# Experts in nine weight slots, and one body for all rounds of an expert in nested fixed loops

## The reference

```python
g_star = argmax(xf @ wg + bg)                   # one of 4 groups
e_logits = (xf @ we + be)[group g_star]         # its 8 experts
top_val, top_idx = lax.top_k(e_logits, 2)       # two experts a token
gate = p_group * softmax(top_val)
y_e = (silu(x_e @ w1[e]) * (x_e @ w3[e])) @ w2[e]   # for the tokens of expert e
out = sum over the token's two experts of gate * y_e
x = layer_norm(alpha * x + out)
```

## Time and profile before

| what | value |
|---|---|
| median of 3 runs | 1573.17 us (1564.77 to 1573.19) |
| the profiled execution | 1563.52 us, its span 1561.5 us |
| granted TensorE clock over the span | 0.929 |
| TensorE matmul busy | 1202.1 us (77%) |
| weight loads of the MoE | 192 of 2 MB |
| mean DMA rate over the span | 303 GB/s |

### The profile page before, as it was taken

How to read it: one execution, slowest core, us unless ns; L and a number is a source line. 1 busy time by engine, 2 the same in 40 slices (tenths; PEclk the granted TensorE clock), 3 DMA queues, 4 the chain that set the end, 5 groups by cost and what they waited for, 6 DMA issues and landing times.

```text
span 1561.5 us, 39311 instructions
## 1 busy us (share of the span) xinstructions
PE 1202.1 (77%) x16430; PEld 843.9 (54%) x16431; DVE 385.5 (25%) x1017; ACT 155.0 (10%) x455; POOL 62.1 (4%) x88
## 2 busy tenths in 40 slices
PE   7999999966767767667669999997778666666652
PEld 6884547544545545445547866655555444444431
DVE  1863622251111111112114222252111111111113
ACT  0211401110000000000001001100000000000000
POOL 3000010010000000000001001020000000000001
PEclk9999999988999999989979999989999899998996
DMA  9655113168998999999992445134799999999992
GB/s 322 235 185 193 55 54 135 55 269 363 429 429 357 428 428 429 428 429 429 428 396 84 162 162 188 55 135 163 327 429 428 430 428 429 428 428 430 428 428 92
DMA packets 63203, 473.39 MB, mean 303 GB/s; under 512 B 4092, under 2 KB 9532, under 8 KB 38572
## 3 DMA queue, kind: packets, MB, share of 16 engines
q1 hardware_dynamic: 60940, 465.78, 72.8%
q0 software_dynamic: 2208, 6.81, 1.4%
HBM read 471.52 MB, written 1.05 MB: 303 GB/s over the span
## 4 chain that ended last, share of the span: by engine, by line
PE 51%; DMA 35%; issue 7%; DVE 5%; ACT 1%; POOL 0%; DVEq 0%; SPq 0%; POOLq 0%
DMA ring<-in_moe_w_dram 34%; PE bank L462 13%; PE bank L825 12%; PE bank L475 7%; PE bank L841 4%; PE bank L849 2%; PE bank L817 2%; PE bank L638 2%; DVE x L960 1%; DMA ring<-in_ev_w_in_dram 1%; PE bank L593 1%; PE bank L764 1%; PE bank L437 1%; PE bank L626 1%; ACT prob L1527 1%
## 5 line engine op out<-in xcount | busy, mean ns | idle before, releaser
L825 PE MATMUL bank<-ring,kT 128*32 128x128 f32 x8192 | 307.2, 316 | 217.8 <-DMA ring<-in_moe_w_dram 135.8
L825 PEld LDWEIGHTS bank<-ring,kT 128*32 128x32 f32 x8192 | 272.5, 128 | 258.4 <-DMA ring<-in_moe_w_dram 130.1
L462 PE MATMUL bank<-xT,ring 128*128 128x256 f32 x832 | 181.9, 380 | 4.2 <-DMA ring<-in_ev_w_in_dram 1.6
L462 PEld LDWEIGHTS bank<-xT,ring 128*128 128x128 f32 x832 | 158.0, 191 | 28.4 <-issue 4.7
L841 PE MATMUL bank<-ring,probT 128*32 128x256 f32 x2336 | 140.6, 381 | 32.7 <-DMA ring<-in_moe_w_dram 25.3
L1272 DVE SCALAR_TENSOR_TENSOR probT<-probT,bank 128x128 f32<-128x128 f32 x73 | 21.0, 288 | 493.9 <-ACT probT L1521 493.5
L841 PEld LDWEIGHTS bank<-ring,probT 128*32 128x32 f32 x2336 | 73.5, 109 | 93.2 <-DMA ring<-in_moe_w_dram 44.7
L475 PE MATMUL bank<-ring,oT 128*128 128x512 f32 x256 | 110.8, 593 | 3.8 <-issue 1.9
L849 PE MATMUL bank<-prob 32*128 32x256 f32 x1024 | 74.0, 400 | 32.0 <-ACT prob L1527 31.5
L475 PEld LDWEIGHTS bank<-ring,oT 128*128 128x128 f32 x256 | 48.3, 190 | 64.7 <-issue 64.7
L849 PEld LDWEIGHTS bank<-prob 32*128 32x128 f32 x1024 | 46.5, 184 | 64.6 <-ACT prob L1527 62.3
(11 more groups left out here) (268 smaller groups left out, 935.4 us busy)
## 6 DMA issues: line engine op xcount, KB each, us to landing
ring<-in_moe_w_dram SPq DMA_DIRECT2D x192, 2048.0 KB, 25.4
ring<-in_od_w_in_dram SPq DMA_DIRECT2D x6, 2048.0 KB, 16.2
ring<-in_ev_w_in_dram SPq DMA_DIRECT2D x4, 2048.0 KB, 16.4
ring<-in_xa_wq_dram SPq DMA_DIRECT2D x4, 2048.0 KB, 12.0
ring<-in_xa_wo_dram SPq DMA_DIRECT2D x4, 2048.0 KB, 11.3
ring<-in_mem_wk_dram SPq DMA_DIRECT2D x2, 2048.0 KB, 14.1
ring<-in_mem_wv_dram SPq DMA_DIRECT2D x2, 2048.0 KB, 11.2
ring<-in_ev_w_out_dram SPq DMA_DIRECT2D x2, 2048.0 KB, 7.8
```

The source lines that it names most:

```text
L462: ins = mm(ps, w[:, k, c0:c0 + P], rhs[:, k, :], start=(k == 0), stop=(k == KC - 1))
L825: ins = mm((b1, b3)[m][qs[q], 0:P], xg[:, k, :], w[:, k, q * P:(q + 1) * P], start=(k == 0), stop=(k == KC - 1))
```

## The change

- The six slots of `ring` are joined by three more, laid over buffers that are dead in the MoE: `slot6` over `qT, aT, kT, blocks`, `slot7` over `prob, probT`, `slot8` over `memT, oT`. Three sets of three slots hold three experts. Nine loads are issued ahead of the MoE loop, as each slot comes free (`xa_done` is new for `slot7`).
- The small MoE buffers (`xgT`, `hid`, `disp`, ...) move into `xT`, which is dead in the MoE.
- There is one body for all rounds of an expert, and one family of semaphores a layer. Each engine goes through two nested fixed loops (4 x 2 passes), with a test in each, in place of the first round's code and the loop of 7 passes. The next round, of whatever expert, is always gathered in the middle of the present one.
- An expert's registers `m` (its rounds) and `first` (the rounds ahead of it) are loaded before its rounds. They come from `units`, which is made by a comparison, a reduction and two small matmuls instead of the prefix sum.
- The tail behind TensorE's loop is gone: the loop has 11 turns of 3 experts, with an empty 33rd expert. The loop's first instruction is put on the start of a block of instructions (`head_slot`).

```diff
-                with pe.Fori(0, TURNS - 1) as i:
-                    for j in range(SETS):
-                        expert(i, j, False)
-                for j in range(SETS):
-                    expert(TURNS - 1, j, j == SETS - 1)
+                def unit(s, ready, n):
+                    pe.wait_ge(fam.gathered, n)
+                    pe.wait_ge(loaded[s[0]], ready[0])
+                    hidden(fam, 0, s[0], xgT)
+                    pe.wait_ge(loaded[s[1]], ready[1])
+                    hidden(fam, 1, s[1], xgT)
+                    pe.wait_ge(fam.disp_gated, n)
+                    turn(fam, dispg)
+                    pe.wait_ge(fam.disp_built, n + 1)
+                    gather(fam, disp)
+                    ...
+                    results(fam, s[2])
+                    pe.wait_ge(fam.y_ready, n)
+                    scatter(fam, comb, y)
+                with nc.Fori(0, TURNS, engines=[pe.engine], head_slot={pe.engine: 0}) as i:
+                    for j in range(SETS):
+                        m, first = load_units(pe, L, i * SETS + j)
+                        ...
+                        with pe.Fori(0, ROUNDS // 2) as ra:
+                            with pe.If(m > ra * 2):
+                                with pe.Fori(0, 2) as rb:
+                                    with pe.If(m > ra * 2 + rb):
+                                        unit(s_, ready, first + ra * 2 + rb + 1)
+                                    pe.nop()
                             pe.nop()
```

The same on VectorE, and SP's loads:

```diff
+                with v.Fori(0, NE) as e:
+                    m, first = load_units(v, L, e)
+                    with v.Fori(0, ROUNDS // 2) as ra:
+                        with v.If(m > ra * 2):
+                            with v.Fori(0, 2) as rb:
+                                with v.If(m > ra * 2 + rb):
+                                    r = ra * 2 + rb
+                                    n = first + r
+                                    with v.If(n > 0):
+                                        v.wait_ge(fam.disp_gated, n)
+                                        build(e, r)
+                                        elements(n)
+                                        v.wait_ge(fam.comb_done, n)
+                                        v.wait_ge(fam.gather_done, n + 1)
+                                        take(fam, xgT)
+                                    v.nop()
+                                    v.wait_ge(fam.disp_built, n + 1)
+                                    weight(e)
+                def next_expert(e, j):
+                    m, first = load_units(sp, L, e)
+                    for m_ in range(3):
+                        s = slots[j][m_]
+                        sp.wait_ge(used_up[m_], first + m)
+                        sp.dma_start(slot_ap(s), expert_weights(PARTS[m_], L, e + SETS)).then_inc(loaded[s], 16)
```

The routing's end on VectorE and TensorE:

```diff
-                st.do(ts(counts[:, 1, :], counts[:, 0, :], float(CAP), None, ALU.is_gt))
-                ... (the prefix sum of L1312 to L1322)
+                st.do(tt(beyond[:, :], banks[7][0:NE, 0:ROUNDS], round_caps[0:NE, :], ALU.is_gt))
+                nc.vector.tensor_reduce(units_of[:, :], beyond[:, :], AX, ALU.add).then_inc(units_of_ready, 1)
+                v.wait_ge(fam.gather_done, 1)
+                take(fam, xgT)
+                v.wait_ge(first_ready, L + 1)
+                cp(units[0:1, L, :, 0:NE], ...).then_inc(units_ready, 1)
...
+                pe.wait_ge(units_of_ready, L + 1)
+                mm(bY[0:1, 64:64 + NE], units_of[:, :], ident[0:NE, 0:NE], start=True, stop=True)
+                mm(bY[0:1, 64 + NE:64 + 2 * NE], units_of[:, :], tri[0:NE, 0:NE], start=True, stop=True).then_inc(first_ready, 1)
+                pe.wait_ge(units_ready, L + 1)
```

More of the change, by code:

```diff
@@ L242, in program @@
         mask_ready = sem("mask_ready")
-        rounds_ready = sem("rounds_ready")
-        held_over = sem("held_over")
-        shift_done = [sem(f"shift_done{L}") for L in range(DEPTH)]
+        xa_done = sem("xa_done")
+        counted = sem("counted")
+        units_of_ready = sem("units_of_ready")
+        first_ready = sem("first_ready")
+        units_ready = sem("units_ready")
         class Family:
@@ L307, in wait_drained, with load_units @@
             eng.wait_ge(bank_drained[b], n)
[L309 to L314, removed]
+        def load_units(eng, L, e):
+            at_ = bass.ds(e, 1) if not isinstance(e, int) else slice(e, e + 1)
+            m = eng.value_load(units[0:1, L, 0, at_], min_val=0, max_val=ROUNDS)
+            first = eng.value_load(units[0:1, L, 1, at_], min_val=0, max_val=UNITS - 1)
+            return m, first
         block = ctx.enter_context(nc.Block())
@@ L322, in _, with wait_free @@
             at = [0]
+            def wait_free(s):
+                last = slot_last[s]
+                if last is None:
+                    return
+                if len(last) == 2:
+                    sp.wait_ge(last[0], last[1])
+                else:
+                    m, first = load_units(sp, last[1], last[2])
+                    sp.wait_ge(last[0], first + m)
             def load(key, dst_view, src):
@@ L326, in load @@
                 at[0] += 1
-                last = slot_last[s]
-                if last is not None:
-                    sp.wait_ge(last[0], last[1])
+                wait_free(s)
                 slot_uses[s] += 1
@@ L387, in _ @@
                     load_out(f"xo{L}{'ab'[h]}", T["xa_wo"][L], 512 * h)
[L389 to L392, removed]
+                free = [(at[0] + k) % RING for k in range(RING)]
+                slots = ((free[0], free[1], 6), (free[2], free[3], 7), (free[4], free[5], 8))
@@ L393, in _ @@
+                moe_slots.append(slots)
                 moe_base.append(list(slot_uses))
-                sp.wait_ge(rounds_ready, L + 1)
-                e0 = L * NE
-                with sp.Fori(1, TURNS) as i:
-                    for j in range(SETS):
[L399 to L405, removed]
@@ L406, in _ @@
-                for j in range(SETS):
[L407 to L414, removed]
+                slot_last[6] = (weights_used, order.index(f"wo_mix{L}b") + 1)
@@ new lines, in _ @@
+                sp.wait_ge(units_ready, L + 1)
+                with sp.Fori(0, TURNS - 2) as i:
+                    for j in range(SETS):
+                        next_expert(i * SETS + j, j)
+                for e in range((TURNS - 2) * SETS, NE - SETS):
+                    next_expert(e, e % SETS)
+                for e in range(NE - SETS, NE):
+                    for m_ in range(3):
+                        s = slots[e % SETS][m_]
+                        slot_uses[s] += e // SETS + 1
+                        slot_last[s] = (used_up[m_], L, e)
@@ L777, in _ @@
                     wait_drained(pe, ("xo", L, h))
+                pe.nop().then_inc(xa_done, 1)
                 out_projection(f"xo{L}", 3 * L + 1)
@@ L851, in scatter @@
                     ins.then_inc(fam.scattered, 1)
-                e0 = L * NE
+                fam = families[L]
                 for t in range(TT):
                     pe.wait_ge(x_ready[t], 3 * L + 2)
[L856 to L887, removed]
-                                    pe.wait_ge(main.gathered, n1 + 1)
-                                pe.wait_ge(fam.disp_built, k1)
-                                gather(fam, more_disp)
-                                pe.wait_ge(fam.gathered, k1)
-                                hidden(fam, 0, 3 * j, more_xgT)
-                                hidden(fam, 1, 3 * j + 1, more_xgT)
-                                pe.wait_ge(fam.disp_gated, k1)
-                                turn(fam, more_dispg)
-                                pe.wait_ge(fam.comb_ready, k1)
-                                pe.wait_ge(fam.hidT_ready, k1)
-                                results(fam, 3 * j + 2)
-                                pe.wait_ge(fam.y_ready, k1)
-                                scatter(fam, more_comb, more_y)
-                            pe.nop()
-                        pe.nop()
@@ L1303, in _ @@
                 st.wait()
-                v.wait_ge(main.disp_built, e0 + 1)
-                weight(main, disp, dispg, 0)
-                v.wait_ge(main.gather_done, e0 + 1)
-                take(main, xgT)
-                v.wait_ge(main.disp_gated, e0 + 1)
-                build(main, disp, place_of(place, 1))
-                wait_drained(v, ("pos", L))
-                st.do(ts(counts[:, 1, :], counts[:, 0, :], float(CAP), None, ALU.is_gt))
-                for r_ in range(2, ROUNDS):
-                    st.do(stt(out=counts[:, 1, :], in0=counts[:, 0, :], scalar=float(r_ * CAP), in1=counts[:, 1, :], op0=ALU.is_gt, op1=ALU.add))
@@ L1369, in _ @@
-                with v.Fori(0, TURNS - 1) as i:
-                    for j in range(SETS):
-                        expert(i, j, 2)
-                for j in range(SETS):
-                    expert(TURNS - 1, j, SETS - 1 - j)
```

(5 more changed lines are left out.)

231 lines of the change are left out of this document (108 added, 123 removed).

## The result

The changed kernel takes 1658.12 us (median of 4 runs, 1648.38 to 1661.0) against 1572.66: the ratio is 1.055 (95% interval 1.051 to 1.060), slower. Its profiled execution has a span of 1646.4 us against 1561.5, 84.9 more.

What follows compares the result with a forecast made beforehand. Weight transfers were taken to bound the MoE, TensorE being only a little faster; after the change TensorE would, at 15.7 us an expert. Layer 0 +63 and layer 1 +47 on 1563.5 gave 1673, stated as 1675 us, range 1590 to 1725.

Steps and rivals of the forecast that it cites:

- A failing pass: On TensorE's queue, one loop pass whose test fails (add, move, two taken branches) costs 0.735 us; four per one-round expert.
- From `scatter` to `hidden`: TensorE's control between experts, first `scatter` matmul to next `hidden`: 6.73 us, against 2.2 before.
- The slow round: TensorE's way from `hidden` to `scatter` takes 8.95 us instead of 7.29, its clock being lower after each longer gap.
- An expert 15.7 us: TensorE's time per one-round expert, 8.95 + 6.73 us, over the weights' 14.67; bounds 15.2 to 16.4.
- A further round: Another round of the same expert on TensorE costs 7.6 us, following at once; before, 9.85 plus failing passes of 4.4.
- Loop ends: Behind each layer's last expert: loop ends 4 us and an instruction fetch 3.3 us before the first matmul after the loop.
- The routing: Before each layer's experts, TensorE's wait for `units_ready`, loads and loop entries delay first `hidden` by 2.3 us; VectorE adds 4 in layer 0.
- The third set: Nine weight loads instead of six ready when routing ends: 43 + 22 = 65 us to be had if weights stayed the bound.
- Rival (a): TensorE's rounds keep the upper clock, 14.0 us an expert: 1568 us, no change; chance 0.12.
- Rival (b): TensorE's queue hides the control, gap under 3 us, expert under 12, weights stay the bound: 1498 us; chance 0.10.
- Rival (c): Instruction fetches in the expert loop, one miss of 3.3 us an expert, 211 us more: 1885 us; chance 0.06.
- the two rules: Skill's rules set against the trace: a taken branch costs about 108 ns (trace 0.214 us); far branches fetch (none in steady loops).

Runs made afterwards that it cites:

- e3_eight_outer: Changed kernel with TensorE's outer loop at 8 passes instead of 4, the four more always failing; 1847.37 us (one run).
- e4_fill: Changed kernel with three bf16 matmuls on zeros, results unused, at the end of every outer pass of TensorE; 1548.32 us, ratio 0.992.
- e1_loop_of_m: Changed kernel with TensorE's nested loops replaced by one loop of exactly m passes, other engines keeping theirs; 1501.97 us, ratio 0.961 to the kernel before.
- e5_two_sets: e1_loop_of_m with two sets of three slots instead of three; 1526.11 us, ratio 0.975 to the kernel before.
- e6_before_passes: Kernel before the change plus a loop of five failing passes on TensorE at the end of every expert; 1597.33 us, ratio 1.022.

## Why the prediction was right, point by point

The sign, the mechanism and the size held (1675 forecast, 1658 measured, in the range). The sum is 25 us too high: it has 110 us more than before, and the spans are 84.9 apart. Some terms missed in opposite directions.

- *A failing pass, 0.735 us*: confirmed, 0.74 to 0.75 by e3_eight_outer. The changed kernel's own records have the outer passes from 434.4 to 436.7, three periods.
- *From `scatter` to `hidden`, 6.73 us*: 5.96 and 6.00 (means of 31 in each layer). The sum took too much for arithmetic and for the entries: `ra * 2` has no instruction of its own but lies in the one fused record a pass (41 ns), which the price of a pass already holds, so the term of 0.5 comes to nearly nothing, and the entries into both loops took 0.64 (438.5 to 439.1) where the sum has 0.84. Over 62 experts the 0.75 are 46 us.
- *The slow round, 8.95 us*: too low. The first rounds of the experts take 9.32 and 9.33 (means of 32 in each layer); with the further rounds, which follow at once at 7.29, the mean is 9.05 and 9.11. They alternate between 8.6 and 9.9. Over 62 experts the 0.37 are 23 us, which offset half of the item above: that the sum came so near is in part luck. e4_fill shows that it is the clock. The trace of before had shown it only behind further rounds; that the same gap does it every time was the step that carried the sign, and it held.
- *An expert 15.7 us*: 15.4, from `hidden` to `hidden` (mean of the 54 experts that have one round and another expert behind them). The 0.3 x 62 = 19 us cover the 17 by which the two loops are shorter than the sum has them (533.2 and 526.9 against 543.4 and 533.3). The other 8 of the 25 lie outside the loops, where the sum has 4.6 more than before and the trace 3.7 less; the routing did cost about what was forecast (below), and what else moved there stays open.
- *A further round, 7.6 us*: 7.6. The five experts with two rounds in layer 0 take 23.03 us on average (22.74 for expert 8, from 455.15 to 477.89), less the 15.4 of one that has a single round.
- *Loop ends, 4 + 3.3 us*: 8.2 (856.68 to 864.91). The empty 33rd expert, whose loads and failing passes I forgot, is in it.
- *The routing, +2.3 us in each layer*: from the mask's matmul to the first `hidden` 6.88 us (324.81 to 331.69), 4.62 before (327.42 to 332.04): +2.26; in layer 1 it is +2.0. The +4 for VectorE's loops in layer 0 did not come: `gather` waits 0.75 us for `build`, no more, since `build` ran at 337.90 already. That step was wrong. So was the -1.5 and -1.3 for a warm expert 0: its first `hidden` took 5.37 us in both layers, behind 3.64 and 3.36 us of idle time.
- *The DMA share about 0.93*: 0.91 in layer 0. *Waits for weights vanish*: they did.
- *The third set, 65 us to be had*: e1_loop_of_m gave 62 against the kernel before, but e5_two_sets gives only 24 of it to the set. The prediction put the whole under the third set; most of it comes from the rest of the change.
- *Rival (a), rounds at the upper clock, 1568*: that is what e4_fill forces, 1548: lower since the gap is 6.05 us there and not 6.73. *Rival (b), 1498*: not what happens, but its arithmetic is e1_loop_of_m's 1502. *Rival (c)*, fetches in the loop: none seen. The 10 us that the range allowed for first visits did not come either: behind the first three experts the ways from `scatter` to `hidden` are 6.07, 6.09 and 6.35 us. The kernel before had 8.58 and 9.96 behind its first two, part of what the one body saves.
- On the two rules: the taken compare-and-branch is 0.214 us in the changed kernel as well, not the 108 ns of the Trainium skill (Advanced Engine Details and Errata, Control Flow Timing).

The matmuls of the routing's start, of after:

```profile
324.81 0.41 PE L827 MATMUL bank<-mask,tri 128*128 128x32 f32 x2 [0.31 <-DVE mask L1265]
...
338.18 1.07 PE L848 MATMUL bank<-x,xT 128*32 128x256 f32 x16 [0.75 <-DVE xT L1276]
```

and of before:

```profile
327.42 0.41 PE L798 MATMUL bank<-mask,tri 128*128 128x32 f32 x2 [0.31 <-DVE mask L1248]
```

## What to carry to other kernels

Count the branches on the engine that has the least room, not the instructions saved: here one taken branch on TensorE's queue is 0.27 us from its record to the next, so one an expert is worth 0.27 us x 64 = 17 us when TensorE is the bound, and none of it is in the busy times. A loop of exactly as many passes as there is work replaces tests that fail. And price the idle time that control opens by the clock it costs as well as by itself: a gap of 5 us made the next 7.3 us of work take 9.3 on average.

## What the runs showed of the hardware that was not expected

- Gap and slow rounds go together in steps. With 2.3 to 2.7 us from `scatter` to `hidden` (idle 1.1 to 1.6) rounds stay at 7.29; at 4.5 (idle 3.3) nearly all are near 8.9, a few at 9.4 to 9.6; at 6.0 (idle 4.8 to 5.2) they alternate between 8.6 and 9.9, in two kernels of quite different code. With 8.9 (e3_eight_outer) it is no worse: first rounds of 9.3 and 9.2 us on average. e6_before_passes lies in between: its gaps alternate between 3.8 and 4.3 us (idle 2.6 and 3.1), and in the middle of layer 0 the rounds behind the shorter ones mostly take 7.29 us, those behind the longer ones 8.95 and more:

```profile
535.18 3.70 PE L825 MATMUL bank<-ring,kT 128*32 128x128 f32 x128 [2.63 <-issue]
...
546.74 5.37 PE L825 MATMUL bank<-ring,kT 128*32 128x128 f32 x128 [3.13 <-issue]
```

- Parts that no experiment touches move between executions: the first `hidden` of layer 0 starts between 329.3 and 341.7 us in the traces here. Differences of under 10 us between two single traces say nothing until they are located.
